# Stage ends of a two-layer transformer kernel that signal and update per PSUM bank, a feed-forward's first two units run as a pair, and an opening with small loads over two queues

## The chip, the cores and the metric

The kernel runs on one NeuronCore of a Trainium2 chip, as one launch. The metric is the device time in microseconds. TensorE is called PE below, VectorE DVE, ScalarE ACT, GpSimd POOL and SyncE SP.

## The reference

The input is one sequence of 256 tokens with 1024 features. It passes two blocks in turn. The first has two layers, each with a feed-forward, a three-branch mixer and a second feed-forward; the second has an even and an odd layer, each with another mixer and a feed-forward. All of it is float32. Cut to what matters here:

```python
def rms_norm(x, g):
    return x * lax.rsqrt(jnp.mean(x * x, axis=-1, keepdims=True) + EPS) * g

for l in range(2):                                             # first block
    x = x + 0.5 * swiglu(rms_norm(x, ffa_norm[l]), ffa_w_in[l], ffa_w_out[l])
    x = x + mixer(rms_norm(x, mix_norm[l]))                    # three branches, gates, w_out
    x = x + 0.5 * swiglu(rms_norm(x, ffb_norm[l]), ffb_w_in[l], ffb_w_out[l])
for l in range(2):                                             # second block
    x = x + (even_mixer, odd_mixer)[l](rmsnorm(x, mix_norm_g[l]))
    x = x + conv_glu_ffn(rmsnorm(x, ffn_norm_g[l]), w_gate[l], w_up[l], w_down[l])
# swiglu: (silu(h @ gate) * (h @ up)) @ down, with 2816 hidden features
```

So there are ten stages (five with a feed-forward after a mixer or another feed-forward, the very first feed-forward, and four mixers), and each ends by adding a product to `x`.

## The kernel before

**Layout.** `x` lies in SBUF as 8 chunks (`KC`) of 128 features by 256 tokens. All weights come from HBM as one stream of 614 units of 128 x 1024 floats (512 KB). A unit lands in one of 3 `raw` buffers; ACT copies it to `w_hi` (rounded to the type that PE multiplies), DVE writes the rest, `raw - w_hi`, to `w_lo`. This pair of steps is called a split; 6 slots hold split units, and a split is issued 5 units ahead (`AHEAD`). SP loads unit u+3 when the split of unit u is ready. A slot is free again once PE has counted the unit in `unit_used`. Activations are split in the same way into `a_hi` and `a_lo`. Each product is three matmuls: `w_hi` by `a_hi`, `w_hi` by `a_lo`, `w_lo` by `a_hi`. One unit is 8 x 3 = 24 matmuls of 256 columns.

**A stage's end.** The last units of every stage run in `km`: the unit's 8 matrices go to 8 half banks of PSUM (banks 0 to 3), adding up over units. After the last unit, `update` on DVE waits for `unit_used` and adds the 8 pieces to `x` (L921). All engines run their instructions in program order. On DVE the splits up to five units ahead stand in front of `update`.

**The start of a feed-forward** (`ffn_norm` on ACT, `update` with `gain` and `gained_low` on DVE). The norm's scale per token is put in after the first product, so `a_hi` is `x` times the gain alone (L425). ACT takes chunk by chunk `high(c)` and then `square(c)` (L428). DVE interleaves the update of chunk c with `a_lo` of chunk c-2 (L938). PE runs unit 0, waiting per chunk for `a_lo` (`h_ready`), then unit 1 (both in `fm`). POOL meanwhile adds up the 8 squares in 7 steps (L824), each waiting for the one before. When the sum is there, PE takes its mean over features (`ffn_stat`, two 1-column products for the two token halves). DVE scales it (L929), POOL takes the power -1/2 (L815), DVE writes two diagonals (L931, L932), and after unit 2 PE spreads them over the partitions (`ffn_spread`). From this comes the factor of `scaled` (L957), on which the gate, and through it unit 4, the first `down`, depends. Before `scales`, DVE has two more splits to do, of units 5 and 6 (three at the second layer's first feed-forward). The split of unit 6 takes the slot of unit 0 and waits for PE to have used it.

**The start of a mixer** uses `norm`: ACT squares the chunks, PE sums them itself, and the scaled `x` is split only after the scale is known.

**The opening.** SP issues `x` (1 MB), all parameters (662 KB), three raw units and the constants (800 KB) in this order. ACT waits for `x` and the parameters and then loads its table, DVE waits for the parameters and halves some of them.

**The end.** SP stores each chunk of `x` once DVE has updated it (L390).

Of the kernel before, what the change touches and what calls it, by code (L numbers as in the profile page):

```python
# [25 lines left out]
TOK = 256  # L26
# [9 lines left out]
RAW = 3  # L36
# [153 lines left out]
def build(nc, stream, params, consts, late_in, x_in, out):  # L190
    with ExitStack() as ctx:
# [26 lines left out]
        params_loaded, x_loaded, stored = sem("params_loaded"), sem("x_loaded"), sem("stored")  # L218
# [152 lines left out]
        def _(sp):  # L371
            sp.dma_start(x[:], x_in).then_inc(x_loaded, 16)
            sp.dma_start(par[:], params).then_inc(params_loaded, 16)
            for b in range(RAW):
                sp.dma_start(raw[:, b, :], stream[b]).then_inc(raw_loaded[b], 16)
            sp.dma_start(con[:], consts).then_inc(consts_loaded, 16)
            rounds = (UNITS - RAW) // RAW
# [18 lines left out]
        def _(act):  # L396
# [25 lines left out]
            def ffn_norm(t, gain):  # L422
# [7 lines left out]
                if t == 0:  # L430
                    act.wait_ge(x_loaded, 16)
                    act.wait_ge(params_loaded, 16)
                    for c in range(KC):
                        high(c)
                    split(0)
                    for c in range(KC):
                        square(c)
                    for u in range(1, AHEAD):
                        split(u)
                    return  # L440
                for c in range(KC):
                    act.wait_ge(x_ready, 8 * (t - 1) + c + 1)
                    high(c)
                    square(c)
# [441 lines left out]
        def _(dve):  # L886
# [16 lines left out]
            dve.wait_ge(params_loaded, 16)  # L903
            V.tensor_scalar(par[:, 0:N_HALVED], par[:, 0:N_HALVED], 0.5, None, ALU.mult).then_inc(halved, 1)
            dve.wait_ge(halved, 1)
# [9 lines left out]
            def update(t, units, factor, gain=None):  # L915


                dve.wait_ge(unit_used, units)
                for c in range(KC + 2):
                    if c < KC:  # L920
                        V.scalar_tensor_tensor(x[:, c, :], bank(c // 2, (c % 2) * TOK, (c % 2 + 1) * TOK), factor, x[:, c, :],  # L921
                                               ALU.mult, ALU.add).then_inc(x_ready, 1)
                    if gain and c >= 2:
                        gained_low(t, c - 2, gain)
# [10 lines left out]
            def gained_low(t, c, gain):  # L935
                dve.wait_ge(h_hi_ready, 8 * t + c + 1)
                dve.wait_ge(x_loaded if t == 0 else x_ready, 16 if t == 0 else 8 * (t - 1) + c + 1)
# [665 lines left out]
            for u in range(AHEAD):  # L1603
                split(u)
# [590 lines left out]
```

## Time and profile before

| | us |
|---|---|
| median of 3 runs | 2315.04 |
| lowest and highest | 2313.86 to 2315.19 |
| span of the profiled execution | 2314.1 |

The profile gives for the execution that it shows only this span, 2314.1 us, with no other time beside it. The median of the runs is 0.9 us above it.

| engine | busy us | share |
|---|---|---|
| PE | 2095.3 | 91% |
| DVE | 1531.0 | 66% |
| ACT | 1030.9 | 45% |
| POOL | 161.6 | 7% |

The HBM read is 325.57 MB, 141 GB/s over the span. The table shows a kernel in which PE works nearly all the time. A busy PE is not a fast one, though: at its full clock it starts a 256-column matmul every 0.12 us, at the lower level every 0.21 us, and both count as busy. So at the places where PE stood idle one reads the granted clock beside the idle time.

### The profile page before, as it was taken

The page shows a single profiled execution, that of the slowest core. Times are in us where ns is not written, and L with a number is a line of the kernel's source. Part 1 is how long each engine was busy: PE and PEld are TensorE (multiplying, and loading weights), DVE is VectorE, ACT ScalarE, POOL GpSimd, SP SyncE. Part 2 cuts the span into 40 slices and gives each one's busy share as a digit, 9 for nine tenths or more (in the row PEclk, how much of TensorE's full clock was granted, in tenths as well). Part 3 has the DMA queues.
Part 4 walks back from the last instruction along what each step waited for, and adds up shares of the span by engine and source line. Part 5 has one row for each costly group of instructions (what it writes and reads, how often), then busy time and mean ns, then how long its engine had stood idle before and what let it go on. Part 6 is the DMA issues. An engine that isn't in the chain of part 4 may idle for free. (4 is left out here: it accounts for less than half of the span.)

```text
span 2314.1 us, 41463 instructions
## 1 busy us (share of the span) xinstructions
PE 2095.3 (91%) x15830; PEld 2009.1 (87%) x15830; DVE 1531.0 (66%) x2389; ACT 1030.9 (45%) x1593; POOL 161.6 (7%) x124
## 2 busy tenths in 40 slices
PE   6999998869999999999789799998759998959998
PEld 6998978768999899988687699998758998848998
DVE  5566868556665665668665666665966767675665
ACT  4444532444444544445325444444524554644443
POOL 1000003010100000000310001000601000101000
PEclk9999999989999999989899899998969998979999
DMA  5564531123455555545213254554424554513553
GB/s 199 181 186 140 189 130 56 64 91 116 146 178 188 164 173 181 187 140 186 70 37 101 73 166 144 183 180 155 140 70 138 180 181 138 164 53 113 180 188 118
DMA packets 90235, 327.93 MB, mean 142 GB/s; under 512 B 10016, under 2 KB 11040, under 8 KB 89888
## 3 DMA queue, kind: packets, MB, share of 16 engines
q1 hardware_dynamic: 90000, 325.55, 43.6%
q8 instruction: 64, 1.05, 0.2%
q10 hardware_dynamic: 144, 1.11, 0.1%
q14 instruction: 27, 0.22, 0.0%
HBM read 325.57 MB, written 1.05 MB: 141 GB/s over the span
## 5 line engine op out<-in xcount | busy, mean ns | idle before, releaser
L1630 PE MATMUL ps<-a_hi,w_hi 128*128 128x256 f32 x4464 | 1295.7, 290 | 79.3 <-DVE a_lo L1443 17.0
L1630 PE MATMUL ps<-a_lo,w_hi 128*128 128x256 f32 x4464 | 1278.3, 286 | 0.0
L1630 PE MATMUL ps<-a_hi,w_lo 128*128 128x256 f32 x4464 | 1277.6, 286 | 0.0
L1630 PEld LDWEIGHTS ps<-a_hi,w_hi 128*128 128x128 f32 x4464 | 872.0, 195 | 100.4 <-issue 20.6
L1630 PEld LDWEIGHTS ps<-a_lo,w_hi 128*128 128x128 f32 x4464 | 873.5, 196 | 1.2 <-issue 0.5
L1630 PEld LDWEIGHTS ps<-a_hi,w_lo 128*128 128x128 f32 x4464 | 872.4, 195 | 0.0
L912 DVE TENSOR_TENSOR w_lo<-raw,w_hi 128x1024 fp32r<-128x1024 f32 x614 | 751.5, 1230 | 144.7 <-ACT w_hi L412 143.9
L412 ACT ACTIVATE w_hi<-raw 128x1024 fp32r<-128x1024 f32 x614 | 635.9, 1051 | 291.8 <-DMA raw<-stream 176.6
L957 DVE TENSOR_TENSOR arena<-ps,arena 128x512 f32<-128x512 f32 x132 | 91.2, 691 | 343.5 <-PE ps L1630 343.3
L449 ACT ACTIVATE arena<-arena 128x256 f32<-128x256 f32 x88 | 36.9, 420 | 261.0 <-DVE arena L957 260.7
L815 POOL TENSOR_TENSOR sc<-sc,nhalf 128x2 f32<-128x2 f32 (+5 forms) x25 | 54.6, 2188 | 1313.0 <-DVE sc L929 805.8
L453 ACT ACTIVATE a_hi<-arena 128x256 fp32r<-128x256 f32 x132 | 55.2, 418 | 127.3 <-DVE arena L966 100.0
L1630 PE MATMUL ps<-w_hi,a_hi 128*128 128x512 f32 (+2 forms) x232 | 89.1, 384 | 5.9 <-DVE a_lo L945 3.6
L1630 PE MATMUL ps<-arena 128*128 128x128 f32 (+4 forms) x400 | 74.9, 348 | 16.7 <-ACT arena L782 7.2
L656 ACT ACTIVATE arena<-arena,par 128x256 f32<-128x256 f32 x44 | 26.5, 602 | 142.1 <-DVE arena L957 142.1
L1630 PE MATMUL ps<-w_lo,a_hi 128*128 128x512 f32 (+2 forms) x232 | 88.3, 381 | 0.0
L1630 PE MATMUL ps<-w_hi,a_lo 128*128 128x512 f32 (+2 forms) x232 | 88.1, 380 | 0.0
L1630 PEld LDWEIGHTS ps<-arena 128*64 128x64 f32 (+2 forms) x400 | 51.2, 183 | 34.5 <-issue 8.0
L824 POOL TENSOR_TENSOR tmp<-tmp 128x256 f32<-128x256 f32 x42 | 33.6, 799 | 539.1 <-ACT tmp L428 534.0
L496 ACT ACTIVATE gates<-ps 128x256 f32<-128x256 f32 x48 | 18.3, 382 | 111.4 <-PE ps L1630 111.4
L971 DVE TENSOR_TENSOR a_lo<-arena,a_hi 128x256 fp32r<-128x256 f32 x132 | 55.2, 418 | 6.3 <-ACT a_hi L453 6.3
L1630 PEld LDWEIGHTS ps<-w_hi,a_hi 128*128 128x128 f32 x232 | 44.9, 193 | 14.8 <-issue 7.7
(286 smaller groups left out, 1620.8 us busy)
## 6 DMA issues: line engine op xcount, KB each, us to landing
raw<-stream SPq DMA_DIRECT2D x614, 512.0 KB, 3.7
gates<-late ACTq DMA_DIRECT2D x1, 1088.0 KB, 6.1
x<-x_in SPq DMA_DIRECT2D x1, 1024.0 KB, 5.1
out<-x SPq DMA_DIRECT2D x8, 128.0 KB, 2.1
con<-consts SPq DMA_DIRECT2D x1, 800.0 KB, 9.9
par<-params SPq DMA_DIRECT2D x1, 662.0 KB, 6.3
```

Of the source, the lines that this page charges most:

```text
L412: nc.scalar.activation(w_hi[:, u % SLOTS, :], raw[:, u % RAW, :], ACT.Copy).then_inc(hi_ready, 1)
L449: nc.scalar.activation(th2[:, p, :], gus[:, p, 0:TOK], ACT.Tanh, scale=0.5).then_inc(gate_act, 1)
L453: nc.scalar.activation(a_hi[:, 8 + p, :], gu2[:, p, :], ACT.Copy).then_inc(gu_hi_ready, 1)
L496: nc.scalar.activation(gates[:, i, :], bank(6 + i % 2, 0, TOK), ACT.Tanh, scale=0.5).then_inc(gate_evac, 1)
L656: nc.scalar.activation(gh2[:, p, :], gus[:, p, 0:TOK], ACT.Identity, scale=w, bias=b).then_inc(conv_in, 1)
L815: return nc.gpsimd.tensor_tensor(o, i, nhalf[:, 0:n], ALU.pow)
L824: nc.gpsimd.tensor_tensor(acc, acc, tmp[:, c, :], ALU.add).then_inc(sq_sum, 1)
L912: V.tensor_tensor(w_lo[:, u % SLOTS, :], raw[:, u % RAW, :], w_hi[:, u % SLOTS, :], ALU.subtract).then_inc(split_ready, 1)
L957: V.tensor_tensor(gus[:, p, :].rearrange("p (a b) -> p a b", b=TOK), bank(4 + p).rearrange("p (a b) -> p a b", b=TOK), each(rrow, 2), ALU. ...
L971: V.tensor_tensor(a_lo[:, 8 + p, :], gu2[:, p, :], a_hi[:, 8 + p, :], ALU.subtract).then_inc(gu_split, 1)
L1630: return nc.tensor.matmul(o, a, b, start=start, stop=stop, **k)
```

## The change

Four things are changed.

1. **Per bank.** In `km`, the last unit of a stage also counts `bank_done` after banks 0, 1 and 2. `update` waits for chunk pair by chunk pair; only the last pair waits for the unit's end. All 8 updates come first, then (before a feed-forward) all 8 `a_lo`.
2. **The pair.** Where a feed-forward follows another stage, `fm_pair` runs units 0 and 1 together: first all products with `a_hi` (32 matmuls, waiting per chunk for `a_hi` alone), then the 16 with `a_lo`. Both units count as used at its end.
3. **ACT's order.** At such a start ACT does all 8 `high`, then all 8 `square`.
4. **The opening.** SP loads first the 8 columns of gains, then half of `x` in two pieces, raw units 1 and 2, the constants and the other parameters. ACT's own queue loads raw unit 0 and the other half of `x`. ACT runs a tiny activation first, which brings the table. The split of unit 0 stands between chunks 3 and 4, ACT's split of unit 1 stands before the squares, and the halving on DVE is moved behind the first five splits.

```diff
@@ sync
-            sp.dma_start(x[:], x_in).then_inc(x_loaded, 16)
-            sp.dma_start(par[:], params).then_inc(params_loaded, 16)
-            for b in range(RAW):
-                sp.dma_start(raw[:, b, :], stream[b]).then_inc(raw_loaded[b], 16)
+            g0 = N_HALVED + WHOLE["ffa", 0][0]
+            sp.dma_start(par[:, g0:g0 + KC], params[:, g0:g0 + KC]).then_inc(gain_loaded, 16)
+            for i in range(2):
+                sp.dma_start(x[:, 2 * i:2 * i + 2, :], x_in[:, 2 * i:2 * i + 2, :]).then_inc(x_loaded[i], 16)
+            sp.dma_start(raw[:, 1, :], stream[1]).then_inc(raw_loaded[1], 16)
+            sp.dma_start(raw[:, 2, :], stream[2]).then_inc(raw_loaded[2], 16)
             sp.dma_start(con[:], consts).then_inc(consts_loaded, 16)
+            sp.dma_start(par[:, 0:g0], params[:, 0:g0]).then_inc(params_loaded, 16)
+            sp.dma_start(par[:, g0 + KC:], params[:, g0 + KC:]).then_inc(params_loaded, 16)
@@ scalar, ffn_norm
                 if t == 0:
-                    act.wait_ge(x_loaded, 16)
-                    act.wait_ge(params_loaded, 16)
+                    act.dma_start(raw[:, 0, :], stream[0]).then_inc(raw_loaded[0], 16)
+                    for i in range(2, KC // 2):
+                        act.dma_start(x[:, 2 * i:2 * i + 2, :], x_in[:, 2 * i:2 * i + 2, :]).then_inc(x_loaded[i], 16)
+                    act.wait_ge(consts_set, 1)
+                    nc.scalar.activation(sc[:, 0:1], ones[:, 0:1], ACT.Copy)
+                    act.wait_ge(gain_loaded, 16)
                     for c in range(KC):
+                        act.wait_ge(x_loaded[c // 2], 16)
                         high(c)
-                    split(0)
+                        if c == 3:
+                            split(0)
+                    split(1)
                     for c in range(KC):
                         square(c)
-                    for u in range(1, AHEAD):
+                    for u in range(2, AHEAD):
                         split(u)
+                    act.wait_ge(params_loaded, 32)
                     return
                 for c in range(KC):
                     act.wait_ge(x_ready, 8 * (t - 1) + c + 1)
                     high(c)
+                for c in range(KC):
                     square(c)
@@ vector, update
-                dve.wait_ge(unit_used, units)
-                for c in range(KC + 2):
-                    if c < KC:
-                        V.scalar_tensor_tensor(x[:, c, :], bank(c // 2, (c % 2) * TOK, (c % 2 + 1) * TOK), factor, x[:, c, :],
-                                               ALU.mult, ALU.add).then_inc(x_ready, 1)
-                    if gain and c >= 2:
-                        gained_low(t, c - 2, gain)
+                for c in range(KC):
+                    if c < KC - 2:
+                        dve.wait_ge(bank_done, 3 * (t - 1) + c // 2 + 1)
+                    else:
+                        dve.wait_ge(unit_used, units)
+                    V.scalar_tensor_tensor(x[:, c, :], bank(c // 2, (c % 2) * TOK, (c % 2 + 1) * TOK), factor, x[:, c, :],
+                                           ALU.mult, ALU.add).then_inc(x_ready, 1)
+                if gain:
+                    for c in range(KC):
+                        gained_low(t, c, gain)
@@ vector, opening
             for c in range(KC):
                 gained_low(0, c, ("ffa", 0))
-            for u in range(AHEAD):
+                if c == 3:
+                    split(0)
+            for u in range(1, AHEAD):
                 split(u)
+            dve.wait_ge(params_loaded, 32)
+            V.tensor_scalar(par[:, 0:N_HALVED], par[:, 0:N_HALVED], 0.5, None, ALU.mult).then_inc(halved, 1)
@@ tensor
+            def fm_pair(u, b, t):
+                s = [(u + q) % SLOTS for q in range(2)]
+                o = [bank(b, q * TOK, (q + 1) * TOK) for q in range(2)]
+                for k in range(KC):
+                    w = slice(k * 128, (k + 1) * 128)
+                    pe.wait_ge(h_hi_ready, 8 * t + k + 1)
+                    for q in range(2):
+                        if k == 0:
+                            pe.wait_ge(split_ready, u + q + 1)
+                        mm(o[q], w_hi[:, s[q], w], a_hi[:, k, :], start=(k == 0 and q == 0), stop=False, skip_group_check=True)
+                        mm(o[q], w_lo[:, s[q], w], a_hi[:, k, :], start=False, stop=False, skip_group_check=True)
+                for k in range(KC):
+                    w = slice(k * 128, (k + 1) * 128)
+                    pe.wait_ge(h_ready, 8 * t + k + 1)
+                    for q in range(2):
+                        i = mm(o[q], w_hi[:, s[q], w], a_lo[:, k, :], start=False, stop=(k == KC - 1), skip_group_check=True)
+                        if k == KC - 1:
+                            i.then_inc(unit_used, 1)
@@ tensor, km
                     i = mm(o, w_lo[:, s, w], a_hi[:, chunk, :], start=False, stop=last, skip_group_check=True)
+                    if last and n % 2 and n < KC - 1:
+                        i.then_inc(bank_done, 1)
@@ tensor, ffn
-                gate_up(0, n0, 0, t)
+                if F0 >= 2:
+                    pe.wait_ge(gs_ready, F0 - 1)
+                if t:
+                    fm_pair(n0, 4, t)
+                else:
+                    fm(n0, bank(4, 0, TOK), 0, t)
+                    fm(n0 + 1, bank(4, TOK, 512))
                 ffn_stat(t)
```

On PE, at the end of units 0 and 1 of the feed-forward that follows the first mixer, the program before has these rows (`ones,tmp` is the product that takes the mean of the squares):

```order
L1630 MATMUL ps<-a_hi,w_hi 128x256
L1630 MATMUL ps<-a_lo,w_hi 128x256
L1630 MATMUL ps<-a_hi,w_lo 128x256
L1630 MATMUL ps<-ones,tmp 128x1 x2
L1630 MATMUL ps<-a_hi,w_hi 128x256
```

At the same place the changed program has:

```order
L1654 MATMUL ps<-a_hi,w_hi 128x256
L1654 MATMUL ps<-a_hi,w_lo 128x256
L1654 MATMUL ps<-a_hi,w_hi 128x256
L1654 MATMUL ps<-a_hi,w_lo 128x256
L1654 MATMUL ps<-a_lo,w_hi 128x256 x16
L1654 MATMUL ps<-ones,tmp 128x1 x2
L1654 MATMUL ps<-a_hi,w_hi 128x256
```

The 16 products with `a_lo` have moved behind all products with `a_hi`; the mean of the squares stands behind them as before.

On ACT, at the start of the same feed-forward, before (first three pairs of eight, then the splits of units 5 and 6 behind the last):

```order
L425 ACTIVATE a_hi<-x,par 128x256
L428 ACTIVATE tmp<-x 128x256
L425 ACTIVATE a_hi<-x,par 128x256
L428 ACTIVATE tmp<-x 128x256
L425 ACTIVATE a_hi<-x,par 128x256
```

And in the changed program:

```order
L418 ACTIVATE w_hi<-raw 128x1024 x8
L431 ACTIVATE a_hi<-x,par 128x256 x8
L434 ACTIVATE tmp<-x 128x256 x8
L418 ACTIVATE w_hi<-raw 128x1024 x2
L464 ACTIVATE arena<-arena 128x256
```

The first square (`tmp<-x`) has moved from the second place to the ninth.

## Rows read from the trace of the kernel before

**Rows 1.** Line L921, the updates: what DVE waited for before it (us, times).
```profile
  PE ps L1630: 8.1, 10
```

**Rows 2.** Timeline of PE, seventh stage's end: start, us, instruction [idle before <-releaser].
```profile
1737.82 0.28 PE L1630 MATMUL ps<-a_lo,w_hi 128*128 128x256 f32 x1
1737.94 0.28 PE L1630 MATMUL ps<-a_hi,w_lo 128*128 128x256 f32 x1
1739.89 0.36 PE L1630 MATMUL ps<-a_hi,w_hi 128*128 128x256 f32 x1 [1.67 <-DVE a_lo L938]
...
1750.36 0.50 PE L1630 MATMUL ps<-ones,tmp 128*128 128x1 f32 x4
```

**Rows 3.** Timeline of DVE, the same stretch.
```profile
1736.53 1.23 DVE L912 TENSOR_TENSOR w_lo<-raw,w_hi 128x1024 fp32r<-128x1024 f32 x1 [1.65 <-ACT w_hi L412]
1738.26 1.09 DVE L921 SCALAR_TENSOR_TENSOR x<-ps,x 128x256 f32<-128x256 f32 x3 [0.50 <-PE ps L1630]
1739.26 0.48 DVE L938 SCALAR_TENSOR_TENSOR a_lo<-x,par,a_hi 128x256 fp32r<-128x256 f32 x1
1739.66 0.42 DVE L921 SCALAR_TENSOR_TENSOR x<-ps,x 128x256 f32<-128x256 f32 x1
...
1745.65 1.75 DVE L912 TENSOR_TENSOR w_lo<-raw,w_hi 128x1024 fp32r<-128x1024 f32 x1
```

**Rows 4.** Timeline of ACT, the same stretch.
```profile
1738.71 0.51 ACT L425 ACTIVATE a_hi<-x,par 128x256 fp32r<-128x256 f32 x1 [2.21 <-DVE x L921]
```

**Rows 5.** Timeline of POOL, the same stretch.
```profile
1740.31 6.00 POOL L824 TENSOR_TENSOR tmp<-tmp 128x256 f32<-128x256 f32 x7 [24.49 <-ACT tmp L428]
```

**Rows 6.** Windows, first update to mean, five starts: length, PE busy, clock, DMA, GB/s.
```profile
601.78:613.81 12.03, 10.03 (x49) 0.72 0.27 86
801.08:811.93 10.85, 7.64 (x48) 1.00 0.33 106
...
sum 59.39, PE 47.80; mean PE 9.56
```

**Rows 7.** Windows of POOL's squares (L824) alone: length, POOL busy, clock, DMA, GB/s.
```profile
16.80:21.80 5.00, 4.61 (x3) 1.00 0.57 182
```

**Rows 8.** Windows of PE: length, PE busy, clock, DMA, GB/s.
```profile
26.10:29.60 3.50, 0.21 (x2) 0.82 0.74 242
28.30:35.10 6.80, 5.47 (x23) 0.50 0.38 133
2124.30:2127.50 3.20, 3.12 (x14) 0.50 0.11 18
```

**Rows 9.** Timeline of the opening, all engines.
```profile
8.87 3.30 ACT L425 ACTIVATE a_hi<-x,par 128x256 fp32r<-128x256 f32 x8
...
13.02 2.55 ACT L428 ACTIVATE tmp<-x 128x256 f32<-128x256 f32 x8
...
14.43 0.58 PE L1630 MATMUL ps<-a_hi,w_hi 128*128 128x256 f32 x1 [14.43 <-DVE w_lo L912]
...
15.24 0.41 PE L1630 MATMUL ps<-a_hi,w_hi 128*128 128x256 f32 x1
...
15.45 0.41 PE L1630 MATMUL ps<-a_lo,w_hi 128*128 128x256 f32 x1
...
22.76 0.58 PE L1630 MATMUL ps<-ones,tmp 128*128 128x1 f32 x4 [0.72 <-POOL tmp L824]
```

**Rows 10.** Windows, all engines (PE, PEld, DVE, ACT, POOL busy), clock, DMA share, GB/s.
```profile
5.00:10.00 5.00, 0.00 (x0) 0.00 (x0) 0.90 (x3) 2.41 (x4) 0.00 (x0) 1.00 1.01 414
```

**Rows 11.** Timeline of ACT and of DVE, from 20 us on.
```profile
25.89 1.06 ACT L412 ACTIVATE w_hi<-raw 128x1024 fp32r<-128x1024 f32 x1 [1.15 <-DMA raw<-stream]
...
28.12 0.15 DVE L929 TENSOR_SCALAR sc<-ps 128x2 f32<-128x2 f32 x1
```

**Rows 12.** Timeline of the end, DVE and SP.
```profile
2307.89 2.74 DVE L921 SCALAR_TENSOR_TENSOR x<-ps,x 128x256 f32<-128x256 f32 x8 [4.41 <-PE ps L1630]
2308.34 3.79 SPq L390 DMA_DIRECT2D out<-x  x8
```

## What was predicted from this, before the changed kernel ran

> **What bounds the kernel now.** I read the page first. PE is busy 91% of the span, so only the places where PE stands still or runs at its lower clock are worth anything to this change: ten stage ends, the opening and the end. Then I read who waits for the updates. DVE stands idle before them for 8.1 us in all, ten times [rows 1], of which 4.41 us belong to the very last [rows 12]. So the wait that the per-bank signals remove is small, about 0.4 us a stage. What holds PE at a feed-forward's start is the row of steps behind it: the last matmul of the seventh stage starts at 1737.94, the next at 1739.89, behind `a_lo`, and the mean of the squares stands at 1750.36, though 48 matmuls at 0.12 us make 5.8 us [rows 2]. From the first update to the mean the five starts take 59.39 us in all; four show both clocks, the one at 801.08 the full one alone, and it is the shortest, 10.85 us [rows 6].
>
> **The start of a feed-forward, step by step.** Times are from the first update of before (1738.26) [rows 3].
>
> *Update.* The last unit takes 24 x 0.12 = 2.9 us, so bank 0 is ready 2.2 us before its end. But the split of unit 4 stands ahead of the update on DVE, from 1736.53 for 1.23 us [rows 3]. The update can start when that one lets go, about 0.5 us earlier than before, at -0.5. It gives no more than DVE's idle time there.
>
> *High parts.* ACT starts 0.45 us after the update [rows 3, 4], so at -0.1, and takes 3.30 us for eight [rows 9]. PE follows the first after some 0.65 us, at 0.5. Four matmuls a chunk are 0.48 us, more than ACT's 0.41, so PE runs through its 32 in 3.8 us, to 4.4.
>
> *Low parts.* Updates go at 0.34 us, eight until 2.2; then `a_lo` at 0.40 us each while POOL is quiet [rows 3]. PE has the first five in hand at 4.4. The last three run beside POOL and take about 0.9 us, POOL's own step being 0.86 [rows 5]; the last is there at 7.0. The pair ends at 7.4. Before it ended at 12.1. That is 4.7 us off PE, at the full clock.
>
> *Squares.* Now the cost. Before, POOL began its sums 2.05 us after the first update and took 6.00 for seven [rows 5], to 8.05, in the shadow of the slow pair. Now the squares stand behind eight `high`: they begin at -0.1 + 3.3 = 3.2, the second is ready 0.7 later, and POOL begins at 3.9. Undisturbed it would end at 9.9. But the splits of units 5 and 6 on DVE now fall inside its seven sums: unit 5 behind the last `a_lo` at about 7, unit 6 after the pair's end (7.4, then ACT's 1.06 us), at about 8.7. What such a meeting costs I read in the opening, where the splits of units 1 to 3 ran beside the sums: three sums took 4.61 us there, 1.54 each [rows 7], against 6.00 / 7 = 0.86 with the gap between them [rows 5]. In the other direction a split that begins just behind a sum takes 1.75 us instead of 1.23 [rows 3]. So each split that falls between two sums adds 0.8 to 1.1 us to the row. Two of them: 1.9. POOL ends at 11.8 and the mean stands at 11.85. At the second layer's first feed-forward three splits stand there, 12.8.
>
> The Trainium skill says the same more sharply (SBUF — State Buffer, Who interferes with whom): a DVE instruction with two SBUF inputs and a GpSimd one that reads SBUF exclude each other, and the one that comes second blocks until the first is through. By that rule alone each split would add its whole 1.23 us, so 12.4 instead of 11.85; the rows show somewhat less, and they decide. It speaks against the new order, which puts the sums under the splits.
>
> *Sum to the mean.* 4 x 11.85 + 12.8 = 60.2 us against 59.4 [rows 6]: +0.8. The 4.7 us that PE wins turn into a wait for POOL from 7.4 to 11.85, a gap of 4.5 us.
>
> *Clock.* The granted clock after a gap: at 26.10 PE stood still 3.5 us, and from 28.30 to 35.10 it had 0.50, that is 1.2 instead of 2.4 GHz; at 2124.30 it was down for 3.2 us [rows 8]. A gap of 4.5 us is longer than that of 3.5, so I expect the fall at nearly every one of the five. Unit 2 has 24 matmuls; at 0.21 apiece [rows 9] against 0.12 it takes 2.2 us more, and the spread stands behind unit 2. Where the clock comes back in its middle it costs 1.2. I take 1.85: 5 x 1.85 = 9.3. Ends: 0 (clock held) and 2.75 each (half of 5.5 us, since in [rows 8] the clock stayed down from 29.6, where PE went on, to 35.1). Before, the slow time lay in the pair and is in the 59.4.
>
> Feed-forward starts together: +0.8 + 9.3 = +10.1, ends about -8 (below) and +14.6.
>
> **The start of a mixer.** Four times the update starts as soon as the splits let go. DVE's idle there is (8.1 - 4.4 - 5 x 0.5) / 4 = 0.3 [rows 1, 3, 12]; squares follow the updates one by one. 4 x 0.3 = -1.2; bounds 0 and -2.
>
> **The end.** The eight stores start 0.47 us apart, 3.79 in all, from 2308.34 [rows 12]. With the banks signalled, six updates and their stores lie under the last unit. Update 6 still waits for the unit, 2307.89; its store starts at 2308.35, the last at 2308.85. Before, it started at 2311.7. -2.8; no work hides anything behind it. Bounds -2 and -3.2.
>
> **The opening.** Before, ACT begins at 8.87, behind all of `x` and the parameters, PE at 14.43, behind the split of unit 0 [rows 9]. Data comes at 414 GB/s [rows 10], 0.41 MB a us, from about 2.5 us on. Two queues share this: I give each half. ACT's holds 0.5 + 0.5 MB, so raw unit 0 is there at about 5.6, the last of `x` at 8; SP's first half of `x` at 5.5. ACT: chunks 0 to 3 until 6.4, split of unit 0 until 7.5, the rest until 9.1. DVE's split ends at 8.7 and PE starts at 8.8, 5.6 us earlier. This does not reach the end whole. The squares begin at 10, the sums at 10.8 instead of 13.9, beside the splits again, so the mean stands near 19 instead of 22.76 [rows 9]. `scales` stood at 28.12 behind the split of unit 6, whose load ACT had waited for until 25.89 [rows 11]. That load is the last of a chain in which each load waits for a split and each split for a load. The chain's first load, of unit 3, waits for the split of unit 0, 5.6 us earlier; it then stands behind the 4.1 MB of the opening, which are through at 2.5 + 4.1 / 0.41 = 12.5, still before 14.43. Its later links meet the sums on DVE, which gain only 3 to 4 us. Between 5.6 and 3.8 I take -4.9, so `scales` at 23.2. Bounds: -2 (loads delay each other over two queues) and -6. The halving and the late parameters hide behind the wait for unit 5.
>
> **Edits at nothing.** Three more counts per last unit ride on matmuls. The pair frees unit 0's slot only at its end, 7.4; unit 6's split is not needed before the fifth unit is done, so that hides.
>
> **Sum.** -4.9 - 1.2 - 2.8 + 10.1 = +1.2 us on the shown execution's 2314.1, so 2315.3. The median of the runs lies 0.9 above that span: 2316.2. Measurement can tell about 0.2% (4.6 us) from no change.
>
> **Rivals.**
>
> *A, the clock holds.* PE's gap costs itself alone: 10.1 becomes 0.8, the sum -8.1, time 2307. For it: at 801.08 PE was idle for 10.85 - 7.64 = 3.2 us in pieces, and the clock stayed at 1.00 [rows 6]. Against it: 3.5 us in one piece did not leave it there [rows 8]. 0.2.
>
> *B, the sums run undisturbed*, because DVE's splits come later than I place them. The mean stands at 10.0 five times: 50 - 59.4 = -9.4. The gap is then 2.6 us; the clock costs perhaps 1.3 each, +6.5. With the rest -11.8, time 2303. For it: before, seven sums took 6.00 beside `a_lo` [rows 5]. Against it: the split of unit 5 is in DVE's queue right behind the last `a_lo`. 0.15.
>
> *C, slower.* One mechanism: after the gap the clock stays down through unit 2 and into unit 3, as from 29.6 to 35.1 in the opening. 5 x 2.75 + 0.8 = +14.6, sum +5.7, time 2320.7. It decides from a loss of 2.6 us a start on; at less the forecast holds. For it: that one long stretch; against: at 2124.3 it was 3.2 us. 0.17.
>
> *D, the change doesn't do what it says*, since splits stand before the update and no bank signal is ever early. That is half in the forecast. Beyond it only the end could lose its 2.8: time 2319. 0.03.
>
> **How the numbers follow.** The forecast has 0.45, its own range 2311 to 2319. Faster by over 0.2% (below 2310.4): A's 0.17 of 0.2, B's 0.15, a tail 0.03 of the forecast: 0.35. Slower (above 2319.7): 0.12 of C, 0.06 of the forecast's tail and D: 0.18. Within: 0.47. The range that holds 8 in 10 reaches from half of B to C: 2304 to 2321.
>
> **What would show it.** Right: at the five starts PE's row has the 32 high products dense from some 0.8 us after the stage's last matmul; a wait of 4 to 5 us of PE before `ones,tmp` released by POOL L824's line; POOL sums of 1.5 us beside `w_lo`; windows behind the mean at a clock near 0.5. The opening's first matmul near 9, `scales` near 23; the last store 1 us after the last update. Wrong: the mean within 10.5 us of the first update, or a clock of 1.00 behind it, would give A or B; an opening with `scales` later than 26 would cost 3 us more.

## The result, and the profile after

The changed kernel takes 2323.43 us (median of 6 runs, 2321.47 to 2326.21), beside it the kernel before 2315.11 (6 runs, 2313.86 to 2319.63). The ratio is 1.0037, with a 95% interval of 1.0026 to 1.0049. It is slower by 8 us where 2316 was forecast, outside the range of 2304 to 2321. The profiled execution spans 2322.5 us instead of 2314.1.

The page's busy times after:

```profile
PE 2095.6 (90%) x15830; PEld 2015.6 (87%) x15830; DVE 1533.6 (66%) x2389; ACT 1031.4 (44%) x1594; POOL 170.9 (7%) x124
```

PE is as busy as before over the whole span, so this row doesn't say where the 8 us are: a place with more standing still and one with more work at the lower clock can hide each other in it. POOL is busy 9.3 us more with the same work, which is the first sign that its sums meet something.

Line L935, the updates, and what DVE waited for before it (answers to [rows 1]):

```profile
  PE ps L1654: 1.1, 1
```

The wait that the bank signals were to take away is gone, 8.1 us to 1.1. What stands behind it is the seventh stage's end, which answers to [rows 2 to 5]. Timeline of PE (rows between left out):

```profile
1742.89 0.28 PE L1654 MATMUL ps<-a_hi,w_lo 128*128 128x256 f32 x1
1743.69 0.36 PE L1654 MATMUL ps<-a_hi,w_hi 128*128 128x256 f32 x1 [0.52 <-issue]
...
1750.04 0.50 PE L1654 MATMUL ps<-a_lo,w_hi 128*128 128x256 f32 x2 [0.38 <-DVE a_lo L957]
1754.81 1.02 PE L1654 MATMUL ps<-ones,tmp 128*128 128x1 f32 x4 [4.28 <-POOL tmp L839]
...
1756.05 0.41 PE L1654 MATMUL ps<-a_lo,w_hi 128*128 128x256 f32 x1
```

Timelines of ACT, POOL and DVE in the same stretch:

```profile
1743.08 3.31 ACT L431 ACTIVATE a_hi<-x,par 128x256 fp32r<-128x256 f32 x8 [1.63 <-DVE x L935]
1746.30 2.55 ACT L434 ACTIVATE tmp<-x 128x256 f32<-128x256 f32 x8
```

```profile
1747.08 7.68 POOL L839 TENSOR_TENSOR tmp<-tmp 128x256 f32<-128x256 f32 x7 [26.93 <-ACT tmp L434]
```

```profile
1742.63 2.73 DVE L935 SCALAR_TENSOR_TENSOR x<-ps,x 128x256 f32<-128x256 f32 x8
1745.28 4.70 DVE L957 SCALAR_TENSOR_TENSOR a_lo<-x,par,a_hi 128x256 fp32r<-128x256 f32 x8
1749.90 3.41 DVE L924 TENSOR_TENSOR w_lo<-raw,w_hi 128x1024 fp32r<-128x1024 f32 x2
1755.87 0.16 DVE L944 TENSOR_SCALAR sc<-ps 128x2 f32<-128x2 f32 x1 [2.55 <-PE ps L1654]
...
1761.73 0.42 DVE L1017 COPY arena<-ps 128x256 f32<-128x256 f32 x1 [4.40 <-PE ps L1654]
```

Read from the first update at 1742.63. PE restarts after a gap of 0.80 us between starts instead of 1.95 [rows 2] and is through the pair 7.9 us after the update (before: 12.3). But the first square starts at 1746.30, behind eight `high`, POOL begins 4.45 us after the update (before: 2.05) and takes 7.68 us for its seven sums (before: 6.00), the two splits of 3.41 us lying inside them. PE stands still for 4.28 us before the mean, `ones,tmp`, which POOL's line releases. Behind it its matmuls come 0.21 us apart. The window from the mean to the copy of the spread factor, PE (the columns are window, length, PE busy, granted clock, DMA share and GB/s):

```profile
1754.80:1761.73 6.93, 6.92 (x32) 0.54 0.24 79
```

To say where 8 us went one has to cut the span the same way in both kernels. Here the stretch from a stage's last matmul to the copy of the spread factor is called a *start* of a feed-forward (the first `scaled` waits for this copy). The windows of the second of the five and the sum of all five, before and after:

```profile
800.77:815.89 15.12, 11.87 (x83) 1.00 0.46 152
...
sum 80.71, PE 68.94; mean PE 13.79
```

```profile
802.01:820.83 18.82, 12.69 (x83) 0.82 0.46 140
...
sum 92.46, PE 65.66; mean PE 13.13
```

The five starts are longer by 11.75 us, though PE works 3.3 us less in them. The one at 800.77, which had the full clock before, has lost it. The other four had the lower clock in part before too, but while the pair waited for `a_lo` [rows 6]; now it lies behind the wait. Cut at the mean, from the mean to the copy, the second of the five after and then the five together, after and before:

```profile
814.89:820.83 5.94, 5.94 (x32) 0.64 0.46 149
...
sum 31.89, PE 31.88; mean PE 6.38
```

```profile
sum 19.76, PE 19.76; mean PE 3.95
```

So up to the mean the starts take 60.6 us instead of 61.0, and behind it 31.9 instead of 19.8. All of the loss lies behind the mean. The clock doesn't wait for the mean to fall: this is PE in the last part of its wait before the mean at 814.89.

```profile
812.35:814.89 2.54, 0.00 (x0) 0.50 0.71 239
```

At the end DVE and SP read (answers to [rows 12]):

```profile
2316.30 2.91 DVE L935 SCALAR_TENSOR_TENSOR x<-ps,x 128x256 f32<-128x256 f32 x8 [1.07 <-PE ps L1654]
...
2316.76 3.76 SPq L396 DMA_DIRECT2D out<-x  x8
```

The stores begin 1.4 us before the last matmul (2318.14) instead of 0.9 us behind it.

The opening (answers to [rows 9, 11]), all engines:

```profile
6.78 0.91 ACT L431 ACTIVATE a_hi<-x,par 128x256 fp32r<-128x256 f32 x2 [3.12 <-DMA x<-x_in]
8.11 0.91 ACT L431 ACTIVATE a_hi<-x,par 128x256 fp32r<-128x256 f32 x2 [0.42 <-DMA x<-x_in]
...
12.41 2.54 ACT L434 ACTIVATE tmp<-x 128x256 f32<-128x256 f32 x8
...
23.80 1.06 ACT L418 ACTIVATE w_hi<-raw 128x1024 fp32r<-128x1024 f32 x1 [1.84 <-DMA raw<-stream]
```

```profile
11.27 0.58 PE L1654 MATMUL ps<-a_hi,w_hi 128*128 128x256 f32 x1 [11.27 <-DVE w_lo L924]
...
22.32 0.58 PE L1654 MATMUL ps<-ones,tmp 128*128 128x1 f32 x4 [2.52 <-POOL tmp L839]
```

```profile
26.03 0.15 DVE L944 TENSOR_SCALAR sc<-ps 128x2 f32<-128x2 f32 x1
```

PE's first matmul is 3.2 us earlier, but the mean only 0.4 and the scales 2.1. PE now waits 2.52 us before the mean, instead of 0.72 [rows 9].

### The profile page after: what moved, and what is told of

It reads as the page before. It is cut to its first block and busy times, and to the rows that moved or that the text cites. A ratio compares the mean times of both kernels' runs of the same rounds, so it can differ in the third digit from the quotient of the medians.

```text
span 2322.5 us, 41470 instructions
## 1 busy us (share of the span) xinstructions
PE 2095.6 (90%) x15830; PEld 2015.6 (87%) x15830; DVE 1533.6 (66%) x2389; ACT 1031.4 (44%) x1594; POOL 170.9 (7%) x124
## 5 line engine op out<-in xcount | busy, mean ns | idle before, releaser
L839 POOL TENSOR_TENSOR tmp<-tmp 128x256 f32<-128x256 f32 x42 | 42.9, 1022 | 554.6 <-ACT tmp L434 549.4
L1654 PEld LDWEIGHTS ps<-ones,tmp 128*128 128x128 f32 x232 | 37.7, 254 | 35.9 <-POOL tmp L839 23.2
L1654 PE MATMUL ps<-ones,tmp 128*128 128x1 f32 x232 | 38.4, 296 | 32.2 <-POOL tmp L839 24.7
## 6 DMA issues: line engine op xcount, KB each, us to landing
par<-params SPq DMA_DIRECT2D x1, 451.0 KB, 10.1
```

The source lines that it names most:

```text
L839: nc.gpsimd.tensor_tensor(acc, acc, tmp[:, c, :], ALU.add).then_inc(sq_sum, 1)
L1654: return nc.tensor.matmul(o, a, b, start=start, stop=stop, **k)
```

## The experiments

### The order of `high` and `square` on ACT

```diff
                 for c in range(KC):
                     act.wait_ge(x_ready, 8 * (t - 1) + c + 1)
                     high(c)
-                for c in range(KC):
                     square(c)
```

> The changed kernel with ACT's order of before at a feed-forward's start (high, square, high, square). Theory (the price is POOL's late start and its meeting with the splits): POOL's seven sums begin about 2.0 us after the first update instead of 4.45 and take 6.0 instead of 7.7, so the mean of the squares stands about 3 us earlier at each of five starts, and PE's gap in front of it goes from 4.5 to under 1.5 us, so that the clock falls less behind it. 12 to 25 us faster than the changed kernel: 2299 to 2311. Rival (the price is the pair itself, PE's products with a_hi first): the mean stands where it did, within 0.5 us, and the time stays within 4 us of the changed kernel's.

Measured: 2291.84 us (2291.13 to 2297.36, 5 runs), ratio to before 0.9911 [0.9897, 0.9925], more of a gain than was expected. This kernel beats both. It spans 2290.0 us. The five starts, and DVE and POOL at the seventh stage's end, whose last matmul is at 1724.34:

```profile
1724.34:1737.90 13.56, 12.30 (x83) 1.00 0.28 91
...
sum 68.49, PE 61.49; mean PE 12.30
```

```profile
1724.08 2.74 DVE L934 SCALAR_TENSOR_TENSOR x<-ps,x 128x256 f32<-128x256 f32 x8
1726.73 6.15 DVE L956 SCALAR_TENSOR_TENSOR a_lo<-x,par,a_hi 128x256 fp32r<-128x256 f32 x8
```

```profile
1726.13 6.07 POOL L838 TENSOR_TENSOR tmp<-tmp 128x256 f32<-128x256 f32 x7 [23.83 <-ACT tmp L434]
```

POOL begins 2.05 us after the first update again and takes 6.07. Its sums now meet `a_lo` (6.15 us for eight instead of 4.70) and no split. The pair is 1.5 us longer for it, but the mean stands 9.2 us after the update instead of 12.2, right behind the pair, and the clock stays at 1.00. One line of the change costs 24.0 us at the starts (92.46 less 68.49), 31.6 in the medians. Not all of the difference is explained: against the mean span of three executions of the changed kernel (2321.0) 31.0 us are gone, 23.7 at the starts, 5.5 in the mixers and 1.9 in other bodies, which this line doesn't touch. At the starts the loss is ACT's order where the pair is in place; ACT's new order without the pair was not run.

### Work for PE in the gap

The changed kernel, with 36 products that nobody reads, into a bank that is free, between the pair and the mean.

```diff
                     fm_pair(n0, 4, t)
+                    pe.wait_ge(split_ready, n0 + 3)
+                    for i in range(36):
+                        mm(bank(7, 0, TOK), w_hi[:, (n0 + 2) % SLOTS, 0:128], a_hi[:, 0, :])
```

> The changed kernel with 36 products into PSUM bank 7, which nobody reads, between the pair and the mean of the squares, 4.3 us at the full clock in a gap of 4.5. Theory (the gap costs a second time, through the granted clock of unit 2): the windows behind the mean show a clock of 1.00, unit 2 takes 2.9 instead of about 4.7 us, 1.85 us at each of five starts, 9 us in all: about 2314. Rival (the clock behind the gap is not what counts, the factor's chain does): unit 2 is faster, but the factor's first use is no earlier, time within 3 us of the changed kernel's.

Measured: 2307.34 us (2304.8 to 2312.52, 9 runs), 0.9974 [0.9964, 0.9983]. PE's rows around the fill, and the starts' windows:

```profile
1742.47 4.47 PE L1654 MATMUL ps<-a_hi,w_hi 128*128 128x256 f32 x36
1746.96 0.61 PE L1654 MATMUL ps<-ones,tmp 128*128 128x1 f32 x4
```

```profile
1734.98:1751.02 16.04, 15.12 (x119) 1.00 0.31 99
...
sum 81.12, PE 75.67; mean PE 15.13
```

The mean still stands 12.2 us after the first update (1734.71): the wait for POOL is unchanged and only filled. The clock is 1.00 in all five. That alone gives back 11.3 us at the starts (92.46 less 81.12); the medians differ by 16.1, where 9 were expected, and the part beyond the starts is not explained. This is rival A of the prediction, made by hand. That its time comes out too (2307) is in part luck, for the profiled execution took 2310.1, and A's sum also held the opening at -4.9. The run splits the cost of ACT's order at the starts: waiting 12.6 us (81.12 less 68.49), clock 11.3.

### The splits behind the diagonals

```diff
-                split(n0 + AHEAD); split(n0 + 1 + AHEAD)
-                scales(t)
...
+                    V.tensor_scalar(diag[:, 128:256], ident, sc[:, 5:6], None, ALU.mult).then_inc(diag_ready, 1)
+                    split(n0 + AHEAD); split(n0 + 1 + AHEAD)
```

> The changed kernel with DVE's splits of units 5 and 6 behind the two diagonals (the second layer's first feed-forward keeps its third split in front). Theory (DVE's splits stretch POOL's sums): the seven sums take 6.0 instead of 7.7 us at four starts, the mean stands 1.6 us earlier there; in all 5 to 10 us faster than the changed kernel, 2313 to 2318. Rival (POOL's row has its own length there, the meeting costs nothing): the sums take 7.7 us as before and the time stays or grows by the late splits.

Measured: 2311.63 us (2306.95 to 2317.93, 12 runs), 0.9989 [0.998, 0.9998]. POOL and PE at the seventh stage's end, and the starts' windows:

```profile
1742.57 6.11 POOL L839 TENSOR_TENSOR tmp<-tmp 128x256 f32<-128x256 f32 x7 [27.32 <-ACT tmp L434]
```

```profile
1748.73 0.61 PE L1663 MATMUL ps<-ones,tmp 128*128 128x1 f32 x4 [2.70 <-POOL tmp L839]
```

```profile
sum 84.47, PE 65.56; mean PE 13.11
```

With the two splits out of the way POOL takes 6.11 us instead of 7.68: that difference, 1.6 us, is what the meeting cost, as the same sums on the same engine show. The starts win 8.0 us. PE still waits 2.70 us before the mean there, and the clock still falls at all five starts (windows of 0.80 to 0.89). The median is 11.8 us below the changed kernel's and just outside the expected range; the profiled execution, at 2317.93, was the slowest of the twelve.

### The bank signals alone

```diff
-                dve.wait_ge(unit_used, units)
                 for c in range(KC + 2):
+                    if c < KC - 2:
+                        dve.wait_ge(bank_done, 3 * (t - 1) + c // 2 + 1)
+                    elif c < KC:
+                        dve.wait_ge(unit_used, units)
```

This is the kernel before, with this edit (and the signals on PE) alone.

> The kernel before with the per-bank signals alone, updates and a_lo interleaved as before, the rest of before. Theory: the update starts as soon as the splits let go, 0.3 to 0.6 us earlier at nine stage ends, and the last store comes 2.3 to 2.8 us earlier: 5 to 8 us faster than before, 2307 to 2310. Rival (the earlier updates are given back at each start because PE's clock or POOL's sums set it): only the end gains, 2312 to 2313.

Measured: 2305.68 us (2301.69 to 2310.38, 7 runs), 0.9963 [0.995, 0.9976]; span 2307.1. Its starts:

```profile
sum 78.01, PE 68.06; mean PE 13.61
```

Against the mean of three executions of before (the table below) it wins 2.7 us at the starts, 2.0 at the mixers (1086.24 us) and 2.9 at the end, where the first stores lie under the last unit, and 1.2 up to the first stage's end; the other bodies are 2.5 longer. This part of the change is a gain: 5 to 8 us were expected, and the medians give 9.

### The pair undone, in the kernel with ACT's old order

```diff
-                if t:
-                    fm_pair(n0, 4, t)
-                else:
-                    fm(n0, bank(4, 0, TOK), 0, t)
-                    fm(n0 + 1, bank(4, TOK, 512))
+                fm(n0, bank(4, 0, TOK), 0, t)
+                fm(n0 + 1, bank(4, TOK, 512))
```

> The kernel with ACT's old order (e1_order), the pair undone: units 0 and 1 one after the other, each chunk waiting for a_lo. What is left of the change: signals per bank, eight updates before eight a_lo, the opening. Theory (the pair as such is a gain of 2 to 3 us a start, since unit 1 no longer stands behind the last a_lo): the stretch from the stage's last matmul to the factor's copy goes from 13.6 back to about 16 us or more, 10 to 14 us slower than e1_order, 2302 to 2306. Rival (the gain of e1_order comes from the update order alone): within 3 us of e1_order.

Measured: 2309.12 us (2306.26 to 2314.6, 11 runs), 0.9985 [0.9976, 0.9995], against 2291.84 with the pair. PE's first row of the feed-forward, 3.0 us behind the stage's last matmul at 1733.77, and the starts:

```profile
1736.78 0.36 PE L1653 MATMUL ps<-a_hi,w_hi 128*128 128x256 f32 x1 [2.73 <-DVE a_lo L956]
```

```profile
sum 83.33, PE 68.21; mean PE 13.64
```

The pair is worth 14.8 us at the starts (83.33 less 68.49) and 17 in the medians, where 10 to 14 were expected. Without it the new order on DVE, all updates ahead of all `a_lo`, costs time: 83.33 against 78.01 with the bank signals in the old order.

### A later split in the best kernel

The kernel with ACT's old order, with the split of unit 6 behind the diagonals, as in the third experiment, and that of unit 5 left where it is.

> The kernel with ACT's old order (e1_order), and DVE's split of unit 6 behind the two diagonals. In e1_order's trace the mean's scaling waits on DVE for that split until 1735.65, 1.7 us behind the pair's end, and the spread follows unit 2 by 0.69 us. Theory (that split is the next bound): the spread stands right behind unit 2, 0.5 to 0.7 us earlier at each of five starts, 2 to 4 us faster than e1_order, 2288 to 2290. Rival (the late split hides the factor's copy on DVE instead): no gain, 2291 to 2293.

Measured: 2292.36 us (2290.26 to 2292.76, 4 runs), 0.9904 [0.9889, 0.9919]: no faster than 2291.84. That is the rival's number, but not its mechanism: the starts are shorter, and two bodies are longer. First this kernel's windows (the starts' sum, and the bodies of the eighth and the tenth stage), then those bodies without the edit:

```profile
sum 64.90, PE 60.58; mean PE 12.12
```

```profile
1733.38:1922.30 188.92, 184.36 (x1511) 0.98 0.54 174
2098.87:2287.12 188.25, 184.07 (x1512) 0.98 0.49 161
```

```profile
1737.90:1925.13 187.23, 182.68 (x1511) 0.99 0.54 174
2099.86:2285.66 185.80, 181.61 (x1512) 1.00 0.50 161
```

It wins 3.6 us at the starts and loses 4.1 in two bodies whose clock is lower and whose work is the same. That the two go together is what the rows show; why the clock falls there and not in the other kernel stays open.

### The opening of before in the changed kernel

```diff
-            sp.dma_start(par[:, g0:g0 + KC], params[:, g0:g0 + KC]).then_inc(gain_loaded, 16)
-            for i in range(2):
-                sp.dma_start(x[:, 2 * i:2 * i + 2, :], x_in[:, 2 * i:2 * i + 2, :]).then_inc(x_loaded[i], 16)
...
+            sp.dma_start(x[:], x_in).then_inc(x_loaded, 16)
+            sp.dma_start(par[:], params).then_inc(params_loaded, 16)
```

> The changed kernel with the opening of before. Theory (the opening gives 2.6 us up to the factor's copy and about one more behind it): 2 to 5 us slower than the changed kernel, 2325 to 2328. Rival (the earlier start is lost in the first stage): the same time, 2322 to 2324.

Measured: 2325.71 us (2321.29 to 2326.08, 5 runs), 1.0046 [1.0032, 1.006]. The medians differ by 2.3 us from the changed kernel's, and their ranges overlap, so the size is not sharp. The profiles bound it better: DVE's scales stand at 27.79, against 26.03 in the changed kernel, and the first copy of the factor at 30.56, against 28.28 to 29.11 in three executions of it. The new opening is worth 1.5 to 2.3 us, not 4.9.

### `x` ahead of the first weights

```diff
+                    for i in range(2, KC // 2):
+                        act.dma_start(x[:, 2 * i:2 * i + 2, :], x_in[:, 2 * i:2 * i + 2, :]).then_inc(x_loaded[i], 16)
                     act.dma_start(raw[:, 0, :], stream[0]).then_inc(raw_loaded[0], 16)
-                    for i in range(2, KC // 2):
-                        act.dma_start(x[:, 2 * i:2 * i + 2, :], x_in[:, 2 * i:2 * i + 2, :]).then_inc(x_loaded[i], 16)
...
                         high(c)
-                        if c == 3:
-                            split(0)
+                    split(0)
                     split(1)
```

DVE's split of unit 0 moves in the same way.

> The changed kernel with another order in the opening: ACT's queue loads the last half of x first and raw unit 0 behind it, and the split of unit 0 stands behind the eight high parts on both engines. In the changed kernel the first high stood at 6.78 (predicted about 4.4) because x comes in late over two queues beside raw unit 0, PE's first matmul at 11.27, the mean at 22.32, the scales at 26.03. Theory (x's lateness is what cost the opening's gain): with x alone first on both queues, the first high stands 1 us or more earlier, at 5.8 or before, the eight run without idle time to about 9.3, and PE's first matmul stands at 11.0 to 11.5 since the split of unit 0 is now behind all eight; squares at 11.3 instead of 12.41, mean 21.3, scales 25 to 25.5. Rival (a small piece needs some 6 us to land at the start whatever stands behind it, because the queues themselves start slowly): first high unchanged at 6.6 to 6.9, mean and scales within 0.4 of the changed kernel's.

Measured in one run: 2318.7 us, span 2316.9. ACT and DVE in the opening:

```profile
6.57 0.91 ACT L431 ACTIVATE a_hi<-x,par 128x256 fp32r<-128x256 f32 x2 [2.91 <-DMA x<-x_in]
8.46 2.50 ACT L431 ACTIVATE a_hi<-x,par 128x256 fp32r<-128x256 f32 x6 [0.98 <-DMA x<-x_in]
```

```profile
25.49 0.15 DVE L943 TENSOR_SCALAR sc<-ps 128x2 f32<-128x2 f32 x1
```

My theory falls. With nothing but the 4 KB of gains ahead of `x`, its first piece is used 0.2 us earlier, not 1, and the second 0.35 later. So raw unit 0 is not what holds it up, and the rival (a first piece lands late whatever stands behind) fits better. PE starts 2 us later than in the changed kernel (13.22), and the scales are still 0.5 us earlier: PE's early start was not what the scales hung on. Nor did they hang on SP's first wait for a split, which let go at 13.34 here and at 11.40 in the changed kernel. What moved with them is the load of unit 6, for which SP waits until DVE has split unit 3, a split that stands among POOL's sums. SP's row before and in the changed kernel (in this run it stands at 19.58):

```profile
21.33 0.33 SPq L382 DMA_DIRECT2D raw<-stream  x1
```

```profile
19.22 0.33 SPq L388 DMA_DIRECT2D raw<-stream  x1
```

This run is a single one. It is 3.3 us shorter than the second and the third execution of the changed kernel (below); of these 1.3 lie up to the first stage's end, and 1.0 to 1.3 in the first mixer from its scales on (380.5 us against 381.8 and 381.5; the first execution had 384.1), which this edit doesn't touch.

### Both kernels again

The changed kernel and the kernel before, unchanged, two more executions each, since segments that the change leaves alone differed by more than the effects in question.

> The changed kernel once more, unchanged, for a second trace. The four mixers, whose instructions are the same in both kernels, took 1062.8 us in its first trace and 1057.7 in that of before. Theory (the granted clock falls at other places in each execution, whatever the kernel): they come out by 2 us or more away from 1062.8, while the five feed-forward starts repeat at 92.5 within 2. Rival (the change itself lengthens the mixers): 1062 to 1064 again.

> The kernel before once more, unchanged, for a second trace. Its four mixers took 1057.7 us in the first. Theory (the clock falls at other places in each execution): 1055 to 1064, by 1 us or more away from the first; the five starts at 80.7 within 2. Rival (a kernel has its own fixed places): the mixers again within 0.5 us of 1057.7.

> The changed kernel, unchanged, a third look. It is for the four mixers, whose instructions the change leaves as they are: their sum from scales to last matmul was 1057.7 and 1061.3 us in two executions of the kernel before, 1062.8 and 1060.2 in two of the changed one. Theory (where the granted clock falls varies between executions and makes these sums scatter): within 1057 to 1064, and no rule that the changed kernel's lie above. Rival (the changed kernel puts the mixers later against the clock's falls): above 1061.3.

> The kernel before, unchanged, a third look, for the same sums. Theory (scatter): within 1057 to 1064. Rival (the changed kernel is worse in the mixers): below 1060.

Measured: 2322.05 and 2321.95 us for the changed kernel (spans 2320.3 and 2320.2), 2315.05 and 2314.59 for before (2313.3 and 2312.8). The windows from a stage's last matmul to the mixer's last, summed over the four mixers, of the first profile of the changed kernel and of its second:

```profile
sum 1090.43, PE 922.69; mean PE 230.67
```

```profile
sum 1087.68, PE 922.86; mean PE 230.71
```

The same program differs from itself by 2.7 us here. From the scales on alone the four mixers took 1062.8, 1060.2 and 1059.9 us in the changed kernel and 1057.7, 1061.3 and 1056.9 before. The means are 1061.0 and 1058.6, so of the first pair's difference of 5.1 us some 2.3 are left, within ranges that overlap. That the changed kernel is a little worse here (the rival of the last run, below 1060, which 1056.9 meets) is neither shown nor excluded. With the norms added, which the bank signals shorten, the difference is 0.3 us (table).

## Why the prediction was wrong

The terms, against the mean of three profiled executions of each kernel (in brackets each one's figure, us):

| | before | after | measured | predicted |
|---|---|---|---|---|
| opening, to the first copy of the factor, and first body | 214.3 (214.9, 214.0, 213.9) | 211.8 (211.3, 212.1, 212.1) | -2.4 | -4.9 |
| five feed-forward starts | 80.7 (80.7, 80.5, 80.8) | 92.2 (92.5, 92.1, 92.1) | +11.6 | +10.1 |
| four mixers with their norms | 1088.3 (1088.4, 1088.5, 1087.9) | 1088.6 (1090.4, 1087.7, 1087.6) | +0.3 | -1.2 |
| end, from the last matmul | 6.6 | 4.4 | -2.3 | -2.8 |
| other bodies | 923.5 | 924.0 | +0.4 | 0 |
| span | 2313.4 | 2321.0 | +7.6 | +1.2 |

The story held and the sum did not: every gain was put too high and the one loss too low, together 6.4 us in the spans. The median came out 7.2 us above the forecast of 2316.2, and the range left 5.

- **The opening is the largest miss, 2.5 us.** The step that failed is "SP's first half of `x` at 5.5 ... ACT: chunks 0 to 3 until 6.4 ... The squares begin at 10 ... so the mean stands near 19". The first `high` stood at 6.78 and the third at 8.11, the squares began at 12.41, behind eight `high` and two splits, and the mean stood at 22.32, less than 0.5 us earlier than before. I had divided the bytes by half of the full rate for each queue, from 2.5 us on (which gives 5.0 for half of `x`; 5.5 was an allowance that no row gave); the trace has nothing of `x` in use before 6.6 us even when it comes first. The chain of loads was the right frame, but not by its first link: that wait let go 3.2 us earlier, the load of unit 6 started 2.1 us earlier, and 2.1 reached its split and the scales. This was near the bound of -2, and -4.9 was taken. A second thing had no term at all. PE's early start made a wait before the mean here too, 2.52 us in the first execution and 3.54 and 3.65 in the other two. In these two the clock was down through most of unit 2, and the copy of the factor came 3.4 and 3.3 us behind the scales; in the first execution it came 2.25 us behind them.
- **The starts of the feed-forwards: mechanism right, clock too cheap.** POOL was to start 4.4 us after the first update and did at 4.45; the mean was to stand at 12.35 (-0.5 to 11.85) and stood at 12.2; the wait before it was to be 4.5 us and is 4.28. Up to the mean I had +0.8, and measured is -0.4 (60.6 against 61.0). Behind it I had +9.3, and measured is +12.1 (31.9 against 19.8; against the fill kernel's starts as a whole, 11.3). For unit 2 alone the 1.85 a start was right: 15 to 24 of its 24 matmuls ran at the low clock in the first execution, and in the five starts together it takes 9.4 us longer. What had been put at nothing is the mean itself, whose four short products run at the low clock as well and take 0.88 us until unit 2's first matmul instead of 0.36, in five starts 2.6 us. That unit 2's part fits is half luck, for I gave no reason why the clock should come back inside that unit. The rows give one: the low stretch lasted 6.8 us, as in [rows 8], but it began 0.4 to 2.6 us ahead of the mean.
- **The meeting of sums and splits** was to cost 1.9 us a start; taking the splits away shows 1.6, 0.8 a split. The rows used gave 0.7 (1.54 less 0.86), not the 0.8 to 1.1 written. The Trainium skill (SBUF — State Buffer, Who interferes with whom) has the second one blocked until the first is through, which by the splits' own 1.23 us each would be 2.5, an estimate. The trace agrees that DVE's two-input instructions and POOL's sums hold each other up, but by less than that.
- **The mixers' starts** were to win 1.2 us. The wait itself went as forecast: before the fourth mixer DVE's first update stood 0.32 us behind the last matmul (1940.80 against 1940.48), now it stands 0.11 ahead of it (1949.29 against 1949.40), and the four together give some 1.6. From the scales on the mixers are 2.3 us longer in the mean, and single executions scatter by more than that, so whether the whole term is a gain is not settled by these runs.
- **The end** won 2.3 instead of 2.8. I had SP's stores hidden up to the last two. The stores are issued 0.47 us apart from the first one on, 3.76 us in all, and the first can't start before bank 0 is done and updated, 1.4 us before the last matmul: the row of stores is itself the bound. The last of them is issued 1.9 us behind the last matmul, not 1.4.
- **The chances.** Slower by over 0.2% had 0.18. Of this 0.12 was rival C, and it did not happen: the clock came back before the end of unit 2 at four of the five starts, and right behind it at the one whose rows are shown, and the loss was 2.4 us a start, where C needed 2.6. It was the sum of small errors of one sign that did it, the forecast's tail, which had 0.06 together with D. The forecast was also built as a balance of +10 against -9, and its range of 12 us below to 5 above leaned to the side of rivals A and B, which the profile supported only with the one start at 801.08 and with sums that had not yet met a split. The lower end of the starts' own term, "about -8", follows from no sum: rival B's gives -9.4 + 6.5, which is -2.9.

What is shown, and what is only argued: that ACT's order makes the loss at the starts, and how it divides into waiting (12.6) and clock (11.3), is shown by the first two experiments; that the pair and the bank signals are gains, by their own runs. Why the opening's first piece of `x` is used only at 6.6 us stays open, and so does why stages with unchanged instructions shift: single bodies by 1 to 4 us, and the four mixers together from 1088.3 and 1088.6 us in the two kernels to 1083.1 with ACT's old order.

## What to carry to other kernels

When a reordering frees the main engine earlier, ask what feeds its next stop: here the pair ended 4.3 us earlier after the first update, and the row of squares, sums and mean, which had been in its shadow, was at the same time moved 2.4 us back and under the splits. Put the row with the longer tail first (the sum has seven steps behind each square, the product has one), even if the main engine then runs with small holes: the run with ACT's old order had none over 0.7 us at its starts and kept the full clock at all five, while waits of 2.7 us and more lost it at all five. In between the length of a hole doesn't decide: in the kernel before, PE waited 1.67 us at the head of every pair, and the clock fell at four and held at one. And if a forecast is a small difference of large terms, its range must hold their errors with the same sign.

## What the runs showed of the hardware

- A wait of PE of 4.3 us (5.1 at the second) went with a clock of 1.2 GHz over 6.8 us at each of five starts, in all three executions. The low stretch began while PE still stood still, 0.4 to 2.6 us before it went on in the first execution, so even the mean's four products ran slow. The same wait filled with products that nobody reads left the clock at 2.4 GHz, and the kernel won 11 us at its starts for doing more work.
- The clock also falls elsewhere, under unchanged instructions: two executions of one program differed by 2.7 us in the mixers, and an edit that won 3.6 us at the starts lost 4.1 in bodies that it didn't touch.
- POOL's seven sums took 6.0 to 6.1 us with `a_lo` on DVE beside all or part of them, and 7.7 with two splits inside them as well; DVE's eight `a_lo` took 4.7 us with the sums beginning 1.8 us into them, and 6.15 with the sums beside all of them.
